# Two recurrent gates in one half-height product, and a residual scale moved to GpSimd, in a fp32 decoder trunk

## The reference, cut to what matters

```python
h = x * (1 + sc1) + sh1
q, k, v, qi, ki, wi, xr, yg = split(h @ w_in)
# group A: indexer relu(qi . ki) weighted by wi picks 128 causal keys per query; softmax attention over them
# group B:
xc = causal_depthwise_conv(xr)                       # width 4
r = sigmoid(blockdiag(xc, w_gate_a) + b_gate_a)      # 8 blocks of 64 x 64
i = sigmoid(blockdiag(xc, w_gate_x) + b_gate_x)      # 8 blocks of 64 x 64
log_a = -8 * r * softplus(-lam);  a = exp(log_a)
lru = scan(a, sqrt(-expm1(2 * log_a)) * (i * xc)) * gelu(yg)
mix = concat(rms_norm(attn), rms_norm(lru)) @ w_out
x = layer_norm(alpha * x + (1 + g1) * mix)           # first LayerNorm
ff = square(relu((x * (1 + sc2) + sh2) @ w_up)) @ w_down
x = layer_norm(alpha * x + (1 + g2) * ff)            # second LayerNorm
```

## Time and profile before

| | us |
|---|---|
| median of 3 runs | 1291.38 (1291.08 to 1292.97) |
| the profiled execution | 1294.84 |
| its span, first to last instruction | 1293.1 |
| busy: TensorE products | 1255.4 |
| busy: VectorE | 832.9 |
| busy: ScalarE | 541.8 |
| busy: GpSimd | 159.6 |

### The profile page before, as it was taken

How to read it: one execution, slowest core, us unless ns; L and a number is a source line. 1 busy time by engine, 2 the same in 40 slices (tenths; PEclk the granted TensorE clock), 3 DMA queues, 4 the chain that set the end, 5 groups by cost and what they waited for, 6 DMA issues and landing times.

```text
span 1293.1 us, 16839 instructions
## 1 busy us (share of the span) xinstructions
PE 1255.4 (97%) x6036; PEld 994.1 (77%) x6036; DVE 832.9 (64%) x1387; ACT 541.8 (42%) x818; POOL 159.6 (12%) x127
## 2 busy tenths in 40 slices
PE   7999999999999999999999999989999999999996
PEld 5765767787888888888877666778778888888885
DVE  4478995756875765768767999585654353443354
ACT  4643458536513313314245535863462241331331
POOL 0100345110000000001110014501100000000012
PEclk9989999999999999999999999999999999999998
DMA  9953544331554563656224222202133333333321
GB/s 316 308 173 128 164 130 163 115 98 33 183 178 144 172 216 100 226 163 215 84 77 122 75 80 66 81 18 82 34 119 98 94 96 97 97 97 98 98 66 66
DMA packets 78774, 160.66 MB, mean 124 GB/s; under 512 B 6784, under 2 KB 17272, under 8 KB 78712
## 3 DMA queue, kind: packets, MB, share of 16 engines
q1 hardware_dynamic: 66176, 114.90, 28.7%
q0 software_dynamic: 11136, 42.47, 9.8%
q10 hardware_dynamic: 1400, 2.49, 0.8%
HBM read 155.64 MB, written 2.10 MB: 122 GB/s over the span
## 4 chain that ended last, share of the span: by engine, by line
PE 78%; DVE 8%; ACT 6%; issue 3%; DMA 3%; SPq 2%; ACTq 0%; POOL 0%; POOLq 0%; DVEq 0%
PE bank L702 24%; PE bank L704 23%; PE bank L703 23%; PE bank L909 1%; DMA w_raw<-in_w_in_dram 1%; DVE idx_acc L1767 1%; DMA x_in<-in_x_dram 1%; DVE idx_acc L1785 1%; PE bank L583 1%; DMA turned_ring<-xc 1%; PE bank L749 1%; DVE w_lo L1576 1%; ACT a_hi L1082 1%; DVE best L1783 1%; ACT turned_ring L1166 1%
## 5 line engine op out<-in xcount | busy, mean ns | idle before, releaser
L1071 ACT ACTIVATE w_hi<-w_raw 128x1024 fp32r<-128x1024 f32 x192 | 201.9, 1057 | 460.9 <-PE bank L704 451.2
L1576 DVE TENSOR_TENSOR w_lo<-w_raw,w_hi 128x1024 fp32r<-128x1024 f32 x168 | 206.3, 1234 | 252.9 <-ACT w_hi L1071 252.5
L702 PE MATMUL bank<-a_hi,w_hi 128*128 128x512 f32 x896 | 360.1, 402 | 8.0 <-ACT turned_ring L1248 2.9
L704 PE MATMUL bank<-a_hi,w_lo 128*128 128x512 f32 x896 | 350.1, 391 | 0.0
L703 PE MATMUL bank<-a_lo,w_hi 128*128 128x512 f32 x896 | 349.6, 390 | 0.0
L702 PEld LDWEIGHTS bank<-a_hi,w_hi 128*128 128x128 f32 x896 | 168.6, 188 | 67.6 <-issue 26.3
L702 PE MATMUL bank<-b_hi,w_hi 128*128 128x512 f32 x512 | 199.7, 390 | 0.0
L704 PE MATMUL bank<-b_hi,w_lo 128*128 128x512 f32 x512 | 199.3, 389 | 0.0
L703 PE MATMUL bank<-b_lo,w_hi 128*128 128x512 f32 x512 | 199.2, 389 | 0.0
L704 PEld LDWEIGHTS bank<-a_hi,w_lo 128*128 128x128 f32 x896 | 168.6, 188 | 36.2
L703 PEld LDWEIGHTS bank<-a_lo,w_hi 128*128 128x128 f32 x896 | 168.8, 188 | 34.8 <-issue 1.9
(11 more groups left out here) (265 smaller groups left out, 1401.9 us busy)
## 6 DMA issues: line engine op xcount, KB each, us to landing
mod_raw<-in_w_mod_dram POOLq DMA_DIRECT2D x40, 1024.0 KB, 5.9
w_raw<-in_w_up_dram SPq DMA_DIRECT2D x64, 512.0 KB, 3.7
w_raw<-in_w_down_dram SPq DMA_DIRECT2D x64, 512.0 KB, 3.8
w_raw<-in_w_in_dram SPq DMA_DIRECT2D x48, 512.0 KB, 3.7
first_mod<-in_w_mod_dram SPq DMA_DIRECT2D x8, 1024.0 KB, 12.2
w_raw<-in_w_out_dram SPq DMA_DIRECT2D x16, 512.0 KB, 3.7
x_in<-in_x_dram SPq DMA_DIRECT2D x4, 512.0 KB, 11.7
turned_ring<-xc ACTq DMA_DIRECT2D x16, 128.0 KB, 7.0
```

The lines of the kernel that those rows point to most:

```text
L702: mm(o, wh, hi(kk), start=first, stop=False)
L704: last = mm(o, wl, hi(kk), start=False, stop=fin)
L1071: last = af(hi, src, ACT.Copy)
L1576: last = tt(lo, src, hi.bitcast(F32), ALU.subtract)
```

## The change

Both gates of a head come from one pair of half-height products. `blk` holds for each head a 128x128 matrix without zeros: rows 0 to 63 (the even block) have [gate a, gate x] in their columns, rows 64 to 127 (the odd block) [gate x, gate a]. The product of rows 0 to 63 goes to bank 4, that of rows 64 to 127 to bank 5. Each bank then has 64 partitions of gate a, which lie where they belong, and 64 of gate x, which lie on the other half; ScalarE writes these into `gi_swapped` (in yg's buffer) and two DMAs for each two heads move them into `gi`. The bias for them is a copy with the halves exchanged (`bx`). GpSimd and yg's output wait for these DMAs.

The eight scales of the residual behind the first LayerNorm are done by GpSimd (`scaled`), after all 8 `a_lo` tiles.

Besides: the swap of qi is issued in one row of four larger DMAs behind all four banks, with one semaphore, and kiwi's copies follow before the last weight split; VectorE's last low part of xr moves behind the first adds; the indexer pairs of block 1 stand at steps 14, 17, 20 and 23; and no top-k rounds lie between the adds of block 3 (`topk(18)` is dropped and the later calls take more rounds each).

```diff
-        blk = sb("gate_blocks", [P, 2, LT, P])
+        blk = sb("gate_blocks", [P, LT, P])
+        bx = sb("b_gate_x_swapped", [P, LT])
+        gi_swapped = sb("lru_gate_swapped", [P, LT, T], F32, yg_at)
-            gp.memset(blk[:, :, :, :], 0.0).then_inc(p_const, 1)
...
+                        at = 64 * (g ^ par)
+                        pool.dma_start(blk[64 * par:64 * par + 64, :, at:at + 64],
...
                 def gated(m):
-                    pool.wait_ge(free_s[5], uses_before(5, f"gi{m}", l) + 1)
+                    pool.wait_ge(gates_swapped[m // 2], 32 * (l + 1))
...
                         if (name, p) == lows[5]:
-                            for m in range(LT - 1):
-                                gated(m)
+                            gated(0)
+                            gated(1)
                         if (name, p) == lows[7]:
-                            gated(LT - 1)
+                            gated(2)
+                            gated(3)
...
+                def scaled():
+                    pool.wait_ge(a_lo_s, l * 2 * DK + (2 * DK + 2))
+                    for kk in range(DK):
+                        gp.tensor_scalar(x[:, kk, :], x[:, kk, :], gains[:, 6, kk:kk + 1], gains[:, 7, kk:kk + 1],
+                                         ALU.mult, ALU.add).then_inc(x_scaled, 1)
...
                 sums(l * 2)
+                scaled()
...
-                    **dict(zip((14, 17, 19, 21), (idx_pair(1, j) for j in range(IDX_HEADS // 2)))),
+                    **dict(zip((14, 17, 20, 23), (idx_pair(1, j) for j in range(IDX_HEADS // 2)))),
...
-                        for g, (b, name) in enumerate(((4, f"gr{m}"), (5, f"gi{m}"))):
-                            pe.wait_ge(free_s[b], uses_before(b, name, l))
-                            mm(banks[b][:, :], blk[:, g, m, :], xc[:, m, :], start=True, stop=True).then_inc(full_s[b], 1)
+                        pe.wait_ge(free_s[4], uses_before(4, f"gr{m}", l))
+                        pe.wait_ge(free_s[5], uses_before(5, f"gi{m}", l))
+                        for b, rows in ((4, slice(0, 64)), (5, slice(64, P))):
+                            mm(banks[b][:, :], blk[rows, m, :], xc[rows, m, :], start=True, stop=True).then_inc(full_s[b], 1)
...
-                def swap_qi(j):
+                def swap_qi():
                     half = IDX_DH // 2
-                    for m in (2 * j, 2 * j + 1):
+                    for m in range(4):
                         act.wait_ge(free_s[m], uses_before(m, f"qi{m}", l) + 1)
                     for at in range(0, P, half):
                         src = at + half if at % IDX_DH == 0 else at - half
-                        act.dma_start(ring[at:at + half, 2 * j:2 * j + 2, :], xc[src:src + half, 2 * j:2 * j + 2, :])\
-                            .then_inc(qi_swapped[j], 16)
+                        act.dma_start(ring[at:at + half, :, :], xc[src:src + half, :, :]).then_inc(qi_swapped, 16)
...
                         af(xc[:, m, :], banks[m][:, :], ACT.Copy).then_inc(free_s[m], 1)
-                        if m % 2:
-                            swap_qi(m // 2)
+                    swap_qi()
+                    kiwi_copies()
...
                 def yg_out():
+                    for j in range(2):
+                        act.wait_ge(gates_swapped[j], 32 * (l + 1))
...
                 def gate_out(m):
-                    for b, name, dst, bias in ((4, "gr", th, "b_gate_a"), (5, "gi", gi, "b_gate_x")):
-                        act.wait_ge(full_s[b], uses_before(b, f"{name}{m}", l) + 1)
-                        af(dst[:, m, :], banks[b][:, :], ACT.Sigmoid, bias=vcol(bias, m)).then_inc(free_s[b], 1)
+                    at = VEC["b_gate_a"][0] + m
+                    for b, name, r, i in ((4, f"gr{m}", slice(0, 64), slice(64, P)), (5, f"gi{m}", slice(64, P), slice(0, 64))):
+                        act.wait_ge(full_s[b], uses_before(b, name, l) + 1)
+                        af(th[r, m, :], banks[b][r, :], ACT.Sigmoid, bias=vec[r, at:at + 1])
+                        af(gi_swapped[i, m, :], banks[b][i, :], ACT.Sigmoid, bias=bx[i, m:m + 1]).then_inc(free_s[b], 1)
+                    if m % 2:
+                        pair = slice(m - 1, m + 1)
+                        act.wait_ge(free_s[4], uses_before(4, f"gr{m}", l) + 1)
+                        act.wait_ge(free_s[5], uses_before(5, f"gi{m}", l) + 1)
+                        act.dma_start(gi[0:64, pair, :], gi_swapped[64:P, pair, :]).then_inc(gates_swapped[m // 2], 16)
+                        act.dma_start(gi[64:P, pair, :], gi_swapped[0:64, pair, :]).then_inc(gates_swapped[m // 2], 16)
...
-                    if kk >= DK // 2:
-                        scale_residual(1, range(2 * kk - DK, 2 * kk - DK + 2))
...
+                    step(v_.tensor_copy(bx[0:64, :], vec[64:P, at:at + LT]))
+                    step(v_.tensor_copy(bx[64:P, :], vec[0:64, at:at + LT]))
...
-                slot(l, "xr", (none, qi_cosines, qi_sines))
+                split_lo("xr", l, 0)
+                split_lo("xr", l, 1)
+                qi_cosines()
+                split_lo("xr", l, 2)
+                qi_sines()
...
+                idx_add(1, range(0, 2))
+                split_lo("xr", l, PAIRS - 1)
+                idx_add(1, range(2, 4))
                 split_lo("v", l, 0)
-                idx_add(1, range(0, 2))
-                idx_add(1, range(2, 4))
+                idx_add(1, range(4, 6))
                 split_lo("v", l, 1)
-                idx_add(1, range(4, 6))
                 idx_add(1, range(6, 8))
...
                 masks()
-                topk(18)
                 split_lo("k", l, 2)
...
-                for p, rounds_ in enumerate((22, 26, 30, 34)):
+                for p, rounds_ in enumerate((19, 24, 29, 34)):
```

More of the change, by code:

```diff
@@ L297, in trunk_kernel @@
         gate_in = sem("gate_in")
+        gates_swapped = [sem(f"gates_swapped{j}") for j in range(2)]
         xn_ready = sem("xn_ready")
@@ L303, in trunk_kernel @@
         ff_sq = sem("ff_squared")
-        rope_done, qi_cos, qi_swapped = sem("rope_done"), sem("qi_by_cosine"), [sem(f"qi_swapped{j}") for j in range(2)]
+        rope_done, qi_cos, qi_swapped = sem("rope_done"), sem("qi_by_cosine"), sem("qi_halves_swapped")
         idx_acc = sem("idx_accumulated")
@@ L475, in _ @@
             gp.memset(ones_d[:, :], 1.0 / D).then_inc(p_const, 1)
-            gp.memset(blk[:, :, :, :], 0.0).then_inc(p_const, 1)
             gp.memset(eps[:, :], LN_EPS).then_inc(p_const, 1)
-            pool.wait_ge(p_const, 7)
+            pool.wait_ge(p_const, 6)
             def layer(l):
@@ L487, in layer @@
                     for par in range(2):
-                        pool.dma_start(blk[64 * par:64 * par + 64, g, :, 64 * par:64 * par + 64],
+                        at = 64 * (g ^ par)
+                        pool.dma_start(blk[64 * par:64 * par + 64, :, at:at + 64],
                                        A[name][l, :, :, :].rearrange("(t two) c d -> two c t d", two=2)[par])\
@@ L855, in layer @@
                         **{8 * s - 5: stage_rest(s) for s in range(1, FIRST_STAGES)}})
-                    pe.wait_ge(p_const, 7)
+                    pe.wait_ge(p_const, 6)
                     late_mod(l, 0)
@@ L1175, in swap_qi, with kiwi_copies @@
                         src = at + half if at % IDX_DH == 0 else at - half
-                        act.dma_start(ring[at:at + half, 2 * j:2 * j + 2, :], xc[src:src + half, 2 * j:2 * j + 2, :])\
-                            .then_inc(qi_swapped[j], 16)
+                        act.dma_start(ring[at:at + half, :, :], xc[src:src + half, :, :]).then_inc(qi_swapped, 16)
+                def kiwi_copies():
+                    act.wait_ge(full_s[4], uses_before(4, "kiwi", l) + 1)
+                    if l == 0:
+                        act.wait_ge(p_sin, 7)
+                    af(kiwi[0:KIWI, :], banks[4][0:KIWI, :], ACT.Copy)
+                    af(kiwi_swapped[0:32, :], banks[4][32:64, :], ACT.Copy)
+                    af(kiwi_swapped[32:64, :], banks[4][0:32, :], ACT.Copy).then_inc(free_s[4], 1)
                 def qi_out():
@@ L1182, in qi_out @@
                         af(xc[:, m, :], banks[m][:, :], ACT.Copy).then_inc(free_s[m], 1)
-                        if m % 2:
-                            swap_qi(m // 2)
+                    swap_qi()
+                    kiwi_copies()
                 act.wait_ge(vec_ready, l + 1)
                 slot(l, "xr", qi_out)
-                act.wait_ge(full_s[4], uses_before(4, "kiwi", l) + 1)
-                if l == 0:
-                    act.wait_ge(p_sin, 7)
-                af(kiwi[0:KIWI, :], banks[4][0:KIWI, :], ACT.Copy)
-                af(kiwi_swapped[0:32, :], banks[4][32:64, :], ACT.Copy)
-                af(kiwi_swapped[32:64, :], banks[4][0:32, :], ACT.Copy).then_inc(free_s[4], 1)
                 def xr_out():
                     act.wait_ge(qi_cos, l * 4 + 4)
-                    for j in range(2):
```

(9 more changed lines are left out.)

## The result

The changed kernel takes 1301.38 us in the median (1300.80 to 1301.83, 4 runs), a ratio of 1.0066 to the kernel before with a 95% interval of 1.0054 to 1.0079: slower, as forecast, but above the forecast's range (1290.0 to 1299.5; 1295.0 named). The profiled run took 1301.66 us, 6.8 more than the profiled run of before.

The account below looks back on a forecast made before the run. TensorE, busy 97% of the span, was taken to bound the kernel. Gates +5.6, swap +1.2, top-k -1.2 and residual scale -2.0 gave +3.6 us on 1291.4: 1295.0 us, range 1290.0 to 1299.5.

Parts of the forecast that it names:

- Gate products: At the gates, each head's two half-height products overlap on the array: 0.46 us saved a pair, 3.7 for eight.
- Head 1: At the second gate pair, TensorE waits for ScalarE to empty both banks of head 0: +1.3 us.
- Start of yg: yg's first products wait for q banks behind ScalarE's added sigmoids and DMA issues: +2.8 us a layer.
- Top-k: Rounds removed ahead of the k group end its waits; layer 1's indexer pair comes later: -0.6 us a layer.
- Residual scale: Behind each first LayerNorm, scales moved off ScalarE end TensorE's wait: about 1.0 us saved a layer, -2.0 together.
- The port rival: GpSimd's eight scales keep VectorE off the shared port, delaying up1: 11.2 us more than the sum, 1306; chance 0.06.
- the gates' term: Gates through the start of yg, with the pairs' saving contained: +2.8 us a layer, +5.6 for two layers.
- a rival at 0.13: New waits at yg or layer 1's indexer pair bring the clock down: +3.1 us, 1298.1; chance 0.13.
- The base: Time of the unchanged kernel to which the sum was added: median 1291.4 us, against 1294.84 for its profiled run.
- The swap: Layer 0's first indexer pair waits 3.6 us, a later 2.35 us wait goes, the clock falls again: +1.2 us.

Follow-up runs that it names:

- Experiment 3: Kernel after with the swap of qi in two halves, a semaphore each, new order kept: 1296.65 us, ratio 1.0027.
- the fill: Matmuls nobody reads placed in TensorE's gate waits: kernel after, pair 1 only, 1301.40 us; with yg's banks too, 1298.05; kernel before with gates alone, both places, 1300.64.
- experiment 2: Other parts without the new gates: kernel after with old gates 1292.88 us; kernel before with scaling alone 1291.34, top-k alone 1291.88, swap with new order 1296.28.
- experiment 1: Kernel before with the gates' change alone, run in two batches: 1306.16 us (ratio 1.0101) and 1301.17 us (1.0068).

## Why the prediction was wrong

**The steps that held.** *Gate products*: from pair 0 to the next product 1.06 us, taken at 1.25; over a longer stretch, from pair 2 to pair 3, it is 5.35 and 5.38 us in the two layers where it was 5.85 and 5.84, so some 0.5 saved a pair, forecast 0.46. *Head 1*: wait forecast 2.5 us, seen 2.54; +1.4 us at the pair against before, forecast 1.3. *Start of yg*: 13.4 us from pair 3 to the fourth bank in both layers, as written, though the four waits there were not 1.1 us each but 0.22, 0.80, 0.86 and 0.86 in layer 0; +3.0 a layer at full clock, forecast 2.8. *Top-k*: -0.65 and -0.75, forecast -0.6 each, the k group's wait and the new 1.35 us at layer 1's pair in it. *Residual scale*: -1.25 and -1.2, forecast -1.0 each; in the run of it alone the median fell by 1.6, forecast 2.0. The GpSimd operations take 1.86 us each in the mean, where 1.2 was taken between 0.6 and 2.37. The port rival fell: the two engines took turns. VectorE's first low part beside them took 1.69 us, the other two 2.35 together, where one takes 1.22; GpSimd's first scale took 0.77 us and its second, beside the low parts, 3.83. TensorE waited for none of it.

**The step that failed: the gates' term, sized at ScalarE's waits alone.** The forecast charged a fall of the clock where it had seen one, at layer 0's indexer wait, and put none behind the waits that the change adds; that stood as a rival at 0.13, with 3.1 us, and the kernel went that way and further. In the profiled run three falls lie behind new waits, two behind pair 1, at which even the rival did not look, and they make 6.0 us into 10.0: from pair 0 to pair 3 it is 21.5 and 20.3 us, where the profiled run of the gates alone at full clock took 19.9 and 18.7, so 1.6 a layer, and the fall at yg costs 0.9 more. Over the runs of all kernels (225, each against the mean of its kernel in its batch) a run takes 0.82 us more for each .001 of granted clock that it has less, with six tenths of the scatter explained. After's runs lie some .005 under before's: an estimate of 4 us, by a mean in which the end of the run counts too.

**The base, a second error.** The three runs shown of before had a median of 1291.38; in the four batches it was 1293.0 to 1293.8. The sum was made on a profiled run of 1294.84 and then carried over to the lower median, with the guess that those runs had no fall. Their spread is just that: 33 runs of before lie between 1291.2 at a clock of .996 and 1296.0 at .993. The base was 1.5 to 2 us low. So the 6.4 us between 1295.0 and 1301.4 are 1.5 to 2 of base, some 4 of clock, and less than one of everything else.

**The swap** was forecast at +1.2 with a fall on both sides, and the waits came nearly so (4.20 for 2.35); the trace has +0.5, since the slow stretch behind the new wait is shorter than the earlier trace rows. What was not seen is that the two edits of that step pull apart: the new order removes the old wait, the single semaphore makes the new one, and with halves neither is there. Experiment 3 shows it.

**What stays open.** That the falls come with TensorE's new waits is shown by the count over the profiled runs: each fall ahead of a run's end lies in or just behind a wait, and at the gates none is left where the waits are filled. That the fill returns all of the time isn't shown: it gave 0, 3.3 and 0.5 us in three trials, where 0.82 us for each .001 of clock regained would be 0.9, 3.1 and 2.0. Whether a given wait brings a fall was not to be told beforehand: 2.35 us did in the earlier trace rows, 2.88 us did not in experiment 2, the same 1.8 us in layer 1 did and did not. The Trainium skill, TensorE: Matmul & The Clock Gate, section What's actually happening, says that the gate's judgement runs freely and isn't restarted by the kernel; that agrees with one program giving falls in different places (in experiment 1's two profiled runs one lies at 816 us, the other at 80), though no run here shows the gate's own timing. And whether the parts add can't be said: measured alone they come to +8 or +13 (the gates in two batches) + 3 - 1.3 - 1.6, so to +8 or +13, and together to +8.5.

## What to carry to other kernels

On a TensorE-bound kernel like this one a new wait of one to three microseconds had two prices, itself and, in some executions, a fall of the clock behind it: put an expected share of a fall beside each new wait, and take the base and the spread from runs whose granted clock you know. When an operation is split over halves of the array, count first what empties the banks: here ScalarE took as long for 64 partitions as for 128, so two halves cost twice. And where one edit has an order and a semaphore in it, price them apart; one may be the gain and the other the loss.

## What the hardware showed

- A ScalarE sigmoid of 64x512 out of PSUM takes 0.67 to 0.68 us, one of 128x512 0.68 to 0.69. The Trainium skill, TensorEngine Tiling (Array Packing), Performance Considerations, warns that tiling doesn't speed up the emptying; here the emptying took twice the time, since the two halves of a bank went to different places.
- GpSimd's scale and add of 128x512 fp32 with two pointer operands took 0.77 to 3.83 us beside a working VectorE, 1.86 in the mean of eight; VectorE's 128x1024 subtraction meanwhile took 1.69 us once and about 1.2 twice, against 1.22.
- One program's median moved by 5 us between two batches (1306.16, 1301.17), the mean of its granted clock from .9888 to .9915.
- Eight DMAs of two tiles each, the last issued at 62.6 us, were all landed at 72.4; four of four tiles, the last issued at 60.8, at 74.6.
